# Last strip of each gated feed-forward: turned, rounded and split by token tile instead of for both tiles at once

## The reference

```python
def swiglu(x, w_gate, w_up, w_down):
    return (jax.nn.silu(x @ w_gate) * (x @ w_up)) @ w_down
...
    x = x + FFN_RESIDUAL_WEIGHT * rmsnorm(f, ffn2_post_g[l])
```

## Time and profile before

| | |
|---|---|
| median of 3 runs | 1955.32 us (1955.3 to 1955.58) |
| profiled execution, its own time | 1952.88 us |
| its span, first to last instruction | 1951.2 us |
| mean granted TensorE clock (1 is 2.4 GHz) | 0.996 |
| instructions | 27090 |

### The profile page before, as it was taken

The page is one execution under the profiler, slowest core; times in us unless marked ns, Lnnn a source line. Parts: engine busy times, 40 slices in busy tenths (PEclk is TensorE's granted clock), DMA queues, the critical chain, the costliest instruction groups (busy, mean ns, idle before and its releaser), DMA issues.

```text
span 1951.2 us, 27090 instructions
## 1 busy us (share of the span) xinstructions
PE 1911.4 (98%) x9394; PEld 1548.5 (79%) x9394; DVE 1094.0 (56%) x2918; ACT 1039.5 (53%) x1762; POOL 1581.9 (81%) x1160
## 2 busy tenths in 40 slices
PE   9899999999999999999999999999999999999999
PEld 7787777888788777788877877778888787778887
DVE  6556455544554555454455587539654577655764
ACT  6344666544644466554456554655446544556543
POOL 7787775988798877688879777779887968688986
PEclk9999999999999999999999999999999999999999
DMA  6565433666566543367556343456767433346554
GB/s 239 206 211 183 155 126 121 206 193 194 196 229 207 181 164 120 129 209 255 194 185 229 124 142 124 139 166 204 249 194 251 152 120 130 129 131 197 194 194 138
DMA packets 98211, 346.89 MB, mean 178 GB/s; under 512 B 13436, under 2 KB 14108, under 8 KB 97820
## 3 DMA queue, kind: packets, MB, share of 16 engines
q1 hardware_dynamic: 97372, 344.03, 53.3%
q10 hardware_dynamic: 704, 1.14, 0.2%
HBM read 344.08 MB, written 1.05 MB: 177 GB/s over the span
## 4 chain that ended last, share of the span: by engine, by line
PE 85%; POOL 6%; DVE 5%; ACT 3%; issue 1%; DMA 0%; POOLq 0%; SPq 0%; ACTq 0%; DVEq 0%
PE psum L585 26%; PE psum L587 25%; PE psum L586 25%; POOL lo L558 6%; DVE psum L1840 1%; PE psum L755 1%; PE psum L656 1%; PE psum L778 1%; PE psum L765 1%; PE psum L988 1%; PE psum L745 1%; ACT hi L1281 1%; ACT big L1646 1%; DVE big L2425 0%; DVE big L1827 0%
## 5 line engine op out<-in xcount | busy, mean ns | idle before, releaser
L558 POOL TENSOR_TENSOR lo<-raw,hi 128x256 fp32r<-128x256 f32 (+2 forms) x1156 | 1581.7, 1391 | 355.1 <-ACT hi L1281 326.1
L1281 ACT ACTIVATE hi<-raw 128x1024 fp32r<-128x1024 f32 (+1 forms) x616 | 642.9, 1054 | 516.3 <-PE psum L587 482.2
L585 PE MATMUL psum<-hi,h_hi 128*128 128x512 f32 (+1 forms) x1632 | 650.9, 399 | 18.4 <-DVE big L1827 10.1
L587 PE MATMUL psum<-hi,h_lo 128*128 128x512 f32 (+1 forms) x1632 | 636.9, 390 | 0.0
L586 PE MATMUL psum<-lo,h_hi 128*128 128x512 f32 (+1 forms) x1632 | 636.2, 390 | 0.0
L1840 DVE STREAM_TRANSPOSE psum<-big 32x128 f32<-32x128 f32 x1216 | 392.5, 323 | 17.9
L585 PEld LDWEIGHTS psum<-hi,h_hi 128*128 128x128 f32 x1632 | 308.9, 189 | 88.5 <-DVE big L1827 12.2
L587 PEld LDWEIGHTS psum<-hi,h_lo 128*128 128x128 f32 x1632 | 308.0, 189 | 64.9
L586 PEld LDWEIGHTS psum<-lo,h_hi 128*128 128x128 f32 x1632 | 308.8, 189 | 59.4
L585 PE MATMUL psum<-hi,y_hi 128*128 128x512 f32 x832 | 328.2, 394 | 6.0 <-DVE big L2301 4.0
L587 PE MATMUL psum<-hi,y_lo 128*128 128x512 f32 x832 | 324.3, 390 | 0.0
(11 more groups left out here) (263 smaller groups left out, 1294.8 us busy)
## 6 DMA issues: line engine op xcount, KB each, us to landing
raw<-in_stream SPq DMA_DIRECT2D x608, 512.0 KB, 3.5
big<-in_w SPq DMA_DIRECT2D x14, 512.0 KB, 6.4
big<-in_post SPq DMA_DIRECT2D x6, 512.0 KB, 5.1
special<-in_b_merge SPq DMA_DIRECT2D x2, 1536.0 KB, 8.3
raw<-in_stream SPq DMA_DIRECT2D x8, 296.0 KB, 5.6
memkv<-in_mem SPq DMA_DIRECT2D x2, 1024.0 KB, 8.0
big<-in_band SPq DMA_DIRECT2D x2, 768.0 KB, 5.0
x<-in_x SPq DMA_DIRECT2D x2, 512.0 KB, 5.0
```

Of the source, the lines that this page charges most:

```text
L558: t = pool.tensor_tensor(M.lo[:, slot, w], M.raw[:, slot, w], f32(M.hi[:, slot_hi, w]), ALU.subtract)
L585: pe.matmul(out, lhs_hi, rhs_hi, start=start, stop=False)
L587: return pe.matmul(out, lhs_lo, rhs_hi, start=False, stop=stop)
L1281: act.activation(M.hi[:, slot_hi, used], M.raw[:, slot, used], ACT.Copy).then_inc(sem["hi"], 1)
```

## The change

In the last strip of each gated feed-forward, and only there, the work behind the product is cut by token tile m instead of by bank. DVE makes for each m 16 transposes of 64 elements per partition (two feature blocks times 32 columns) into a bank of its own (bank 2 + m), with one event after each 16: 32 transposes in place of 16. ACT makes two roundings of 128x256 in place of one of 128x512, DVE two subtractions of 128x256 in place of one of 128x512. In DVE's program all 32 transposes stand ahead of the first subtraction. PE waits ahead of tile 0's third piece for the part of tile 0 alone, and for the part of tile 1 ahead of tile 1's third piece. `parts_before` counts one part more per gated feed-forward.

```diff
@@ -206,6 +206,11 @@
 
 def flat(a):
     return a.rearrange("p a b -> p (a b)")
+
+
+def by_k(a):
+
+    return a.rearrange("p (k t) -> p k t", k=2)
 
 
 def tiles(a):
@@ -520,10 +525,10 @@
             piece()
 
 
-def halves_before(s):
+def parts_before(s):
 
     gated = L * 2 * FFN_STRIPS
-    return s if s < gated else gated + 2 * (s - gated)
+    return s + s // FFN_STRIPS if s < gated else gated + 2 * L + 2 * (s - gated)
 
 
 def half_width(c):
@@ -637,8 +642,8 @@
             for i, kt in enumerate(kts):
                 if m and i == len(kts) - 1 and turn:
                     turn()
-                if m == 0 and i in ylo:
-                    pe.wait_ge(sem["ylo"], ylo[i])
+                if (m, i) in ylo:
+                    pe.wait_ge(sem["ylo"], ylo[m, i])
                 half_rows(c + i, m, kt, a_hi, a_lo, banks, i == len(kts) - 1)
 
     def turned_tile(src, m, pairs, banks, ready, until):
@@ -717,7 +722,7 @@
                 strip_piece(c + j, j, h_hi, h_lo, 2 if second else 0)
 
         def down(c, s):
-            pe.wait_ge(sem["ylo"], halves_before(s + 1))
+            pe.wait_ge(sem["ylo"], parts_before(s + 1))
             for i in range(kts):
                 rows(c + i, (s - n0) % 2 * kts + i, y_hi, y_lo, (4, 6), s == n0 and i == 0)
 
@@ -732,8 +737,9 @@
             down(c, n0 + strips - 2)
             c += kts
         order = [(strips - s) % 2 * kts + i for s in ((2, 1) if gated else (1,)) for i in range(kts)]
-        done = halves_before(n0 + strips)
-        last_rows(c, order, y_hi, y_lo, (4, 6), turn_next, {0: done - 1, 2: done})
+        done = parts_before(n0 + strips)
+        ylo = {(0, 0): done - 2, (0, 2): done - 1, (1, 2): done} if gated else {(0, 0): done - 1, (0, 2): done}
+        last_rows(c, order, y_hi, y_lo, (4, 6), turn_next, ylo)
         return c + 4
 
     def turn_qk(kind, first=0, end=4):
@@ -1382,9 +1388,16 @@
         def turn(c, s):
             bank = 4 if s == n0 else 2
             act.wait_ge(sem["used"], c)
+            if gated and s == n0 + strips - 1:
+                for m in range(MT):
+                    kt, toks = (s - n0) % 2 * kts, slice(m * P, m * P + P)
+                    act.wait_ge(sem["turned"], parts_before(s) + m + 1)
+                    act.activation(y_hi[:, kt:kt + 2, toks], by_k(psum[:, bank + m, 0:S]),
+                                   ACT.Copy).then_inc(sem["yhi"], 1)
+                return
             for g in range(kts // 2):
                 kt = (s - n0) % 2 * kts + 2 * g
-                act.wait_ge(sem["turned"], halves_before(s) + g + 1)
+                act.wait_ge(sem["turned"], parts_before(s) + g + 1)
                 act.activation(flat(y_hi[:, kt:kt + 2, :]), psum[:, bank + g, :], ACT.Copy).then_inc(sem["yhi"], 1)
 
         project(c, n0)
@@ -1832,6 +1845,16 @@
 
             bank = 4 if s == n0 else 2
             dve.wait_ge(sem["prod"], s + 1)
+            if gated and s == n0 + strips - 1:
+                for m in range(MT):
+                    src = prod_s[:, m, :].rearrange("p (k c) -> p k c", k=2)
+                    dst = by_k(psum[:, bank + m, 0:S])
+                    for b in range(4):
+                        for a in range(4):
+                            t = dve.transpose(dst[32 * b:32 * b + 32, :, 32 * a:32 * a + 32],
+                                              src[32 * a:32 * a + 32, :, 32 * b:32 * b + 32])
+                    t.then_inc(sem["turned"], 1)
+                return
             for g in range(kts // 2):
                 src = prod_s[:, :, S * g:S * g + S].rearrange("p m (k c) -> p k m c", k=2)
                 dst = psum[:, bank + g, :].rearrange("p (k m c) -> p k m c", k=2, m=MT)
@@ -1843,9 +1866,16 @@
 
         def low(s):
             bank = 4 if s == n0 else 2
+            if gated and s == n0 + strips - 1:
+                for m in range(MT):
+                    kt, toks = (s - n0) % 2 * kts, slice(m * P, m * P + P)
+                    dve.wait_ge(sem["yhi"], parts_before(s) + m + 1)
+                    dve.tensor_tensor(y_lo[:, kt:kt + 2, toks], by_k(psum[:, bank + m, 0:S]),
+                                      f32(y_hi[:, kt:kt + 2, toks]), ALU.subtract).then_inc(sem["ylo"], 1)
+                return
             for g in range(kts // 2):
                 kt = (s - n0) % 2 * kts + 2 * g
-                dve.wait_ge(sem["yhi"], halves_before(s) + g + 1)
+                dve.wait_ge(sem["yhi"], parts_before(s) + g + 1)
                 dve.tensor_tensor(flat(y_lo[:, kt:kt + 2, :]), psum[:, bank + g, :],
                                   f32(flat(y_hi[:, kt:kt + 2, :])), ALU.subtract).then_inc(sem["ylo"], 1)
 
```

## The result

The changed kernel takes 1970.2 us (median of 6, 1970.08 to 1972.26) against 1955.45 us (6 runs) of the kernel before: **14.75 us or 0.79% slower, ratio 1.0079, 95% interval 1.0069 to 1.009**. The profiled execution took 1972.23 us with a span of 1970.6. Two executions further down, one of 7420.88 us in experiment 2 and one of 6721.36 us in experiment 3, were disturbed ones in a slow state, and nothing is read from them.

A forecast was written before the change was run, and what follows sets the result against it. The prediction took PE (TensorE, busy 98% of the span) as the bound. It summed 9.0 us of later PE starts and 1.7 us of clock to 10.7 us, so 1955.3 + 10.7 = 1966.0 us, range 1960 to 1971.5.

The forecast's parts named there:

- The transposes: DVE, last strip: 32 of 64 elements at 256 ns take 8.61 us, 3.24 us more per feed-forward.
- Rounding and subtraction: ACT and DVE, last strip: working by tile takes 0.97 us off the path per feed-forward.
- The delay at PE: PE starts the last strip's first piece 2.26 us later per feed-forward, 9.0 us in all.
- The new wait: PE ahead of tile 1's third piece: costs nothing, with over 5 us of cover.
- ACT's and POOL's queues: Work behind ACT's wait for the 32nd transpose moves later but stays covered: ACT by 0.7 us, POOL's by 4.8.
- the second bank: ACT reads bank 2 while DVE writes bank 3: taken as zero, at most 0.4 us per feed-forward.
- The clock: Granted clock after PE's idle 2.76 us: one fall more on balance, 1.7 us; bounds 0 to 6.9, or -3.4.
- The bound of -3.4: Lower bound of the clock term, in us, if the two places that fall today no longer do after the shift.
- proportional transposes: Rival on DVE: transpose time in proportion to elements, 162 ns, whole stall gone, 1952.3 us; chance 0.07.
- transposes no shorter than before: Rival on DVE: 64-element transposes still take 323 ns, 17.6 us more, with falls 1973 to 1980 us; chance 0.08.
- a smaller fixed part: Rival on DVE: 200 to 235 ns each, 1 to 1.6 us per feed-forward, 1959 to 1962 us; chance 0.13.
- the rival with all four falls: Granted clock falls after all four PE waits: 1955.3 + 9.0 + 6.9 = 1971.2 us; chance 0.15.

The follow-up runs named there:

- experiment 2: Kernel before with only the last strip's 16 transposes cut into 32 of 64 elements, one bank, whole rounding and subtraction: 1974.18 us, ratio 1.0097.
- experiment 3: Changed kernel with 16 whole transposes, each writing both banks; rounding and subtraction still by tile: 1952.82 us, ratio 0.999; again 1953.22 us, ratio 0.9992.
- experiment 7: Kernel before with the last strip's transposes cut into 64 of 32 elements: 2003.06 us in one execution.
- experiment 1: Changed kernel with eight unread matmuls ahead of PE's wait for tile 0's part of the last strip: 1964.24 us, ratio 1.0046.
- experiment 4: Changed kernel with tile 0's subtraction moved on DVE ahead of tile 1's 16 transposes: 1970.25 us, ratio 1.0079.
- experiment 6: Experiment 4's kernel with tile 1's rounding made by DVE in place of ACT: 1951.67 us, ratio 0.9985.

## Why the prediction was right, and what in it was off

- **The transposes**: 256 ns and 8.61 us forecast, 256 ns and 8.63 us measured. The slope of the copies, 1.05 ns an element, holds down to 32 elements (experiment 7). The estimate of 223 ns for 64 elements, worked out from the 150 cycles of the Trainium skill, VectorE: DVE Perf Modes, section "The TRN2 errata", is too low: 256 ns were measured, and 223 ns for 32 elements; the measurement decides.
- **Rounding and subtraction**: 0.97 us off the path forecast; between experiment 2 and the change PE's waits differ by 0.95 each. In experiment 3, where no second block of transposes runs beside tile 0's rounding, the gain is 0.49.
- **The delay at PE**: 2.26 us and 9.0 in all forecast; 2.30 and 9.2 in the trace, 8.9 us with the clock held up (experiment 1).
- **The new wait, ACT's and POOL's queues, the second bank**: forecast at nothing; right. PE has no wait ahead of tile 1's third piece, ACT's squares wait for PE, and two banks cost no more (experiments 2 and 3). ACT had the least slack, 0.7 us by the prediction and 0.78 in experiment 1, where the clock is full. It exists only because PE is late: in experiment 4 PE isn't, and the same queue costs 3 us each time.
- **The clock was mis-sized.** The step "I take one fall more on balance, 1.7" measured about 6 us by the medians (14.75 - 8.9) and 10.2 us in the profiled execution. In it the clock fell behind all four places, which the prediction had as a rival at 0.15 (1971.2 us), one fall lasted twice as long (8.5 us in all, not 6.9), and falls at other places added 3.4 on balance, where the sum had other places only as a possible gain. That rows 9 had both longer idle times falling should have weighed more than the remark that some may be spared. The bound of -3.4 counted two present falls; the profile before has four, with 8.6 us of lost clock.
- **The rivals**: proportional transposes and transposes no shorter than before are refuted by 256 ns, and so is a smaller fixed part (for which the sum had a slip: 200 ns would cost 0.5 us each time and not 1). The rule of the Trainium skill, Perfetto Trace Analysis, section "Optimizing Scalar/DVE Operations" (break up instructions where the engine isn't saturated but holds up another), fails for the change as it stands, 1.0079. With the pieces ordered so that the first one is used at once, and tile 1's rounding moved to DVE, the work does end sooner: 0.9985 in experiment 6.

The sum came out at 10.7 us where 14.75 were measured. The path was right to 0.2 us in nine, the clock was not: the 1962 to 1968 us that had most of the chance were missed, and the range of 1960 to 1971.5 holds the median because its top was set by the rival with all four falls. The profiled execution, 1972.23 us, lies above it.

## What to carry to other kernels

Cutting a step in two helps its consumer only if the whole chain of the first half stands ahead of the second half in every engine's queue; count what each engine has queued behind its wait for the second half. Price short instructions by a line through the same engine's rows of several sizes, not in proportion. On a kernel bound by TensorE, add to a longer stall what the granted clock loses behind it, and count a fall for each idle time as long as those that the trace shows followed by one. Falls that merely move can add to that: here 3.4 us on balance.

## What the runs showed of the hardware

The length of an idle time did not decide alone whether the clock fell behind it. In the kernel before PE stood idle for 2.09 us up to 175.54 and kept its clock; in the changed kernel the same wait of the same length, 1.4 us earlier in the span, was followed by a fall:

```profile
174.15 0.63 PE L590 MATMUL psum<-hi,h_hi 128*128 128x512 f32 x1 [2.09 <-DVE big L1840]
```
```profile
174.00:176.00 2.00, 1.85 (x5) 1.46 (x6) 1.90 (x7) 0.00 (x0) 1.65 (x1) 0.59 0.36 141
```

Three more idle times of the changed kernel are followed by a fall where the kernel before had none: 2.10 us up to 678.29, 2.03 up to 1268.85 and 2.36 up to 1740.43 (2.09, 2.02 and 2.00 before). The fall at 1054 is gone, though PE stands idle for the same 2.42 us there. So a shift of the work moves falls that have nothing to do with the change, some 1.7 us each; what decides which idle time is followed by one is not shown.

The kernel before, unchanged, ran in 1952.82 to 1957.03 us over 27 runs. Its granted clock goes with it: 0.996 or 0.997 in the six fastest, 0.992 or 0.993 in all eleven of 1956.0 us or more. The times differ by less than such a difference of the mean clock would make (0.004 of 1951 us is 7.8, against some 3.5), so here too some of the lost clock costs nothing.

Idle times of 2.8 us were followed by a fall at all four places of the changed kernel's profile, and those of 0.99 us at none of the four in experiment 1.
